# Mixer weights split once and kept in DRAM, and hinted back edges of the block loops

## The chip, the cores and the metric

The kernel runs on one NeuronCore of a Trainium2 chip. The metric is the device time of one execution in microseconds; smaller is better.

## The reference

A hybrid encoder block over 4096 rows of width D = 1024, in fp32. A first layer norm (LN0), then a mixer, a layer norm (LN1), a two-level mixture of experts, and a last layer norm:

```
proj = h @ w_in                       # q 512, k 128, v 128, cb/cc/ch 512 each, gates 2 x 1024
y_attn = window_attention(q, k, v) @ w_attn_out      # chunks of 64, 16 meta tokens, ALiBi, sinks
y_conv = (cb * causal_conv3(cc * ch)) @ w_conv_out
mix = (sigmoid(g_a) * y_attn + sigmoid(g_c) * y_conv) @ w_o
h = LN1(alpha * h + mix)
h = LN2(alpha * h + hier_moe(h))      # router, top 2 of 8 experts in the best of 4 groups
```

Only the mixer is touched by the change.

## The kernel before

`mixer` works through the rows in 8 blocks of 512 (TOK), 4 tiles of 128 each. Each fp32 product is made of three fp32r matmuls: both operands are split into a rounded `hi` part and the rest `lo`, and `hi*hi + hi*lo + lo*hi` is summed in PSUM (`product`, L826 to L828).

The weights of a block are 50 strips of 128 x 1024 floats (0.52 MB): k, v, four q (0 to 5), twelve conv strips cc, ch, cb (6 to 17), then for each of the 8 output columns `ga`, `gc`, `out` (18 to 41), then eight `wo` (42 to 49). A strip is 24 matmuls of 512 columns. Strips 0 to 41 write to the two banks `pj` in turn; an `out` strip writes two products, part 0 to the first bank and part 1 to the second, and the strip behind it writes to the first again. ScalarE takes the products of k, v, q, cc, ga and gc out of the banks, VectorE those of ch, cb and out.

Every engine has its own loop over the blocks and in it the 50 iterations written out in order, so the order of an engine's work is fixed in the program:

- SP (SyncE) loads raw strips into 5 buffers (`load`, L451 to L455). In iteration s it waits for `lo_ready`, that is until the strip four back is split, and loads strip s + 1. In iterations 4 to 7 it then waits for the layer norm LN1 of one row tile and stores that tile to `h1` twice. In iterations 26 to 29 (`X_AT`) it waits for `h_copied` and loads one tile of the next block's `x` (L473).
- ScalarE makes the `hi` part of strip s + 1 in iteration s, once strip s - 1 is done (`strip_done`), after the exponentials of an attention unit where there is one (`split_hi`, L517).
- VectorE makes the `lo` part of strip s + 1 in iteration s, behind the layer norms and attention work of that iteration (`split_lo`, L658), and then takes the strip's products. In iterations 26, 29, 32 and 35 (`LN0_AT`) it begins with a wait for a tile of `x` and measures it for LN0 (L41 to L44); only after that come the split and the products of that strip (for `out`: L767, L769, L771, L774). In iteration 7 of every block an `If` on the block number stands in its program.
- TensorE waits for `lo_ready` before each strip and, for strips that write to `pj`, for the bank to be taken (`pj_taken`).
- GpSimd does the scaling of LN1 and LN0 and the copy of `x` rows into `h`.

`strip_done` counts from 2, so a wait for `b * N + s + 3` holds until strip s of block b is done. The splits use 2 `hi` and 2 `lo` buffers. Before the block loop a first stage normalizes the first block's rows and projects the meta tokens with 5 raw buffers; behind it come the last rows' layer norm, `route` and `experts`.

Of the kernel before, what the change touches and what calls it, by code (L numbers as in the profile page):

```python
# [12 lines left out]
P = 128  # L13
# [40 lines left out]
def mixer(nc, t, x, w_in, w_attn_out, w_conv_out, w_o, h1, logits):  # L54
# [37 lines left out]
    RAW = 5  # L92
    assert N % RAW == 0 and N % 2 == 0
# [35 lines left out]
    with ExitStack() as ctx:  # L129
# [6 lines left out]
        raw = sb("raw", [P, RAW, D])  # L136
        w_hi = sb("w_hi", [P, 2, D], F32R)
        w_lo = sb("w_lo", [P, 2, D], F32R)
# [34 lines left out]
        arena = sb("arena", [P, 2 * KD * TOK])  # L173

        def place(at, name, shape, dt=FP32):
            size = 4 * math.prod(shape[1:])
            assert at[0] + size <= shared + 4 * 2 * KD * TOK
            placed = nc.alloc_sbuf_tensor_at(name, shape, dt, offset=at[0])
            at[0] += size
            return placed  # L180

# [27 lines left out]
        with ExitStack() as c1, nc.Block() as block:  # L209
# [4 lines left out]
            raw_in = [sem1(f"meta_raw_in{i}") for i in range(RAW)]  # L214
# [20 lines left out]
            @block.sync  # L235
            def _(sp):
                def load_strip(n):
                    for dst, src in strip_dmas(*meta_strips[n], raw[:, n % RAW, :]):
                        sp.dma_start(dst, src).then_inc(raw_in[n % RAW], 16)
# [6 lines left out]
                for n in range(1, RAW):  # L246
# [12 lines left out]
                for n in range(RAW, len(meta_strips)):  # L259
                    sp.wait_ge(pj_ready, n - RAW + 1)  # L260
                    load_strip(n)
                sp.wait_ge(consts_in, 16 * (7 + TAPS))
# [104 lines left out]
            @block.tensor  # L367
            def _(pe):
                pe.wait_ge(ident_ready, 1)
                pe.wait_ge(ln_done, 1)  # L370
                for k in range(KD):
                    mm = pe.transpose(tp[0][:, k * META:(k + 1) * META], hm[:, k * P:(k + 1) * P],
                                      ident[0:META, 0:META])
                mm.then_inc(tp_ready, 1)
                uses = [0] * RAW
                for what, n in order:
                    if what == "rows":
                        pe.wait_ge(ln_done, n + 1)
                        for half in range(2):
                            q = 2 * (n - 1) + half  # L380
                            pe.wait_ge(tp_taken_dve, max(1, q))
                            for k in range(4):
                                mm = pe.transpose(tp[q % 2][:, k * P:(k + 1) * P],
                                                  xs[:, n - 1, (4 * half + k) * P:(4 * half + k + 1) * P], ident[:, :])
                            mm.then_inc(tp_ready, 1)
                        continue
                    kind, i = meta_strips[n]
                    uses[n % RAW] += 16 * len(strip_dmas(kind, i, raw[:, 0, :]))
                    pe.wait_ge(raw_in[n % RAW], uses[n % RAW])
                    if n == 0:  # L390
                        pe.wait_ge(tp_taken_dve, 1)
                    if n >= 2:
                        pe.wait_ge(pj_taken, n - 1)
                    for k in range(KD):
                        mm = pe.matmul(pj[n % 2][:, 0:META], raw[:, n % RAW, k * P:(k + 1) * P], hmT[:, k, :],
                                       start=(k == 0), stop=(k == KD - 1))
                    mm.then_inc(pj_ready, 1)
# [4 lines left out]
        h1_out = [sem(f"h1_out{i}") for i in range(TILES)]  # L402
        hi_ready = sem("hi_ready")
# [37 lines left out]
        def raw_uses(s, b):  # L441

            per = lambda ss: 16 * len(strip_dmas(*strips[ss], raw[:, 0, :]))
            slot = s % RAW
            in_block = sum(per(q) for q in range(slot, N, RAW))
            return b * in_block + sum(per(q) for q in range(slot, s + 1, RAW))

        with nc.Block() as block:
            @block.sync
            def _(sp):  # L450
                def load(s, b):  # L451

                    hold(sp, lo_ready, b * N + s + 1)
                    for dst, src in strip_dmas(*strips[s % N], raw[:, s % RAW, :]):
                        sp.dma_start(dst, src).then_inc(raw_in[s % RAW], 16)  # L455

                load(0, 0)
                with sp.Fori(0, BLOCKS) as b:
                    for s in range(N):
                        load(s + 1, b)  # L460
# [7 lines left out]
                        if s in X_AT:  # L468
# [4 lines left out]
                            sp.dma_start(xs[:, i1, :], x[bass.ds(nxt * TOK + i1 * P, P), :]).then_inc(x_in[i1], 16)  # L473
                for i1 in range(TILES):
# [37 lines left out]
            def _(a):  # L512
                def split_hi(b, s):
                    uses = raw_uses(s, b) if s < N else raw_uses(0, b + 1)
                    a.wait_ge(raw_in[s % RAW], uses)
                    a.wait_ge(strip_done, b * N + s + 1)
                    a.activation(w_hi[:, s % 2, :], raw[:, s % RAW, :], ACT.Copy).then_inc(hi_ready, 1)  # L517
# [30 lines left out]
                split_hi(0, 0)  # L548
                with a.Fori(0, BLOCKS) as b:
                    for s, (kind, i) in enumerate(strips):  # L550
# [30 lines left out]
                        split_hi(b, s + 1)  # L581
# [15 lines left out]
                        if s in HX_AT:  # L597
# [4 lines left out]
                             .then_inc(hx_hi, 1)  # L602
                for i in range(TILES):
# [6 lines left out]
            def _(v):  # L610
# [19 lines left out]
                def take_logits(b, block_of):  # L630
# [7 lines left out]
                v.sem_inc(lo_ready, RAW)  # L638
# [5 lines left out]
                v.wait_ge(hi_ready, 1)  # L644
                v.tensor_tensor(w_lo[:, 0, :], raw[:, 0, :], w_hi[:, 0, :].bitcast(FP32), ALU.subtract)\
                 .then_inc(lo_ready, 1)
                with v.Fori(0, BLOCKS) as b:
# [7 lines left out]

                    def split_lo(s):
                        v.wait_ge(hi_ready, b * N + s + 1)
                        v.tensor_tensor(w_lo[:, s % 2, :], raw[:, s % RAW, :], w_hi[:, s % 2, :].bitcast(FP32),  # L658
                                        ALU.subtract).then_inc(lo_ready, 1)
# [18 lines left out]
                    for s, (kind, i) in enumerate(strips):  # L678
# [29 lines left out]
                        if 0 <= n < UNITS:  # L708
# [16 lines left out]
                            if n == 1:  # L725
                                with v.If(b == 0):
                                    v.tensor_copy(bias[0:CHUNK, :, META:PREV], bias_prev[:, :, :])\
                                     .then_inc(prev_set, 1)
# [4 lines left out]
                        split_lo(s + 1)  # L733
# [68 lines left out]
                    assert steps[0] == DVE_STEPS  # L802
                v.wait_ge(wo_taken, BLOCKS * 2 * TILES + 1)
# [19 lines left out]
            def _(pe):  # L823
# [35 lines left out]
                with pe.Fori(0, BLOCKS) as b:  # L859
                    pe.wait_ge(hx_lo, b * 2 * TILES + 1)  # L860
                    for s, (kind, i) in enumerate(strips):
# [27 lines left out]
                        pe.wait_ge(lo_ready, b * N + RAW + s + 1)  # L889
# [3 lines left out]
                        if kind == "wo":  # L893
# [5 lines left out]
                            for tt in range(TILES):  # L899
# [3 lines left out]
                                for k in range(2):  # L903
                                    w = slice(k * TOK, (k + 1) * TOK)
                                    mm = product(quad[tt][:, :], mT_hi[:, 2 * kk + k, toks], mT_lo[:, 2 * kk + k, toks],
                                                 w_hi[:, s % 2, w], w_lo[:, s % 2, w],
# [5 lines left out]
                        else:  # L912
# [4 lines left out]
                            for part, (x_hi, x_lo, k0, ks) in enumerate(parts):  # L917
                                no = out_no[(s, part)]
                                pe.wait_ge(pj_taken[no % 2], b * (NOUT // 2) + no // 2 + 1)
                                for k in range(ks):  # L920
                                    w = slice((k0 + k) * P, (k0 + k + 1) * P)
                                    mm = product(pj[no % 2][:, :], w_hi[:, s % 2, w], w_lo[:, s % 2, w],
# [54 lines left out]
                        if s in HX_AT:  # L977
# [8 lines left out]
                            mm.then_inc(hx_ready, 1)  # L986
                pe.wait_ge(hx_lo, BLOCKS * 2 * TILES + 1)
# [677 lines left out]
```

## Time and profile before

| | us |
|---|---|
| median of 3 runs | 4335.98 (4330.54 to 4336.49) |
| profiled execution, its own time | 4333.28 |
| its span | 4331.5 |
| mean granted TensorE clock | 0.988 |

The page of the profile gives busy time by engine and the costliest groups of instructions. A table by stage gives the same for stretches of the span with the granted clock and the DMA traffic. The timeline lists instructions in order of time, with the idle time before each in brackets and what ended it. "issue" there means that the engine waited for nothing that the profile shows.

### The profile page before, as it was taken

To read this page: it belongs to the slowest core of one execution; us is meant where nothing else is said; L and a number is where in the kernel's file an instruction comes from. 1 tells how busy PE (TensorE), PEld (TensorE's weight loads), DVE (VectorE), ACT (ScalarE), POOL (GpSimd) and SP (SyncE) were. 2 spreads that over 40 slices of the span, in tenths; PEclk is the share of its full clock that TensorE was granted. 3 is DMA by queue.
4 is the path that set the end of the run, shared out by engine and by line. 5 is a ranking of instruction groups with operands and counts; after the bars stand their busy time and mean duration, and the time that the engine had idled before them with its cause. 6 is when DMAs were issued, how large, how long until landed. Compare 5 with 4: busy or idle time off the path is not lost. (4 is left out here: it accounts for less than half of the span.)

```text
span 4331.5 us, 62892 instructions
## 1 busy us (share of the span) xinstructions
PE 4171.0 (96%) x20252; PEld 3428.8 (79%) x20253; DVE 2518.7 (58%) x3263; ACT 1773.0 (41%) x2950; POOL 1094.6 (25%) x1117
## 2 busy tenths in 40 slices
PE   7999999999999999999999999499999999999997
PEld 7887887887887888888888887388788888778886
DVE  5555555555555655645645645777666666765664
ACT  2422422422422422422422422466555555654553
POOL 4022032022022021121121121134333333333333
PEclk9999999999999999999999999799999999999998
DMA  6333333333333333333332332187666666765562
GB/s 171 85 107 103 93 102 98 99 104 97 102 104 89 107 106 85 107 104 89 111 102 80 117 102 78 54 289 248 246 199 198 206 199 234 251 203 198 194 204 90
DMA packets 569472, 601.49 MB, mean 139 GB/s; under 512 B 104080, under 2 KB 426640, under 8 KB 569248
## 3 DMA queue, kind: packets, MB, share of 16 engines
q1 hardware_dynamic: 521152, 476.88, 35.5%
q0 software_dynamic: 48096, 121.71, 8.4%
q8 instruction: 130, 2.13, 0.2%
q14 instruction: 94, 0.77, 0.1%
HBM read 527.15 MB, written 124.78 MB: 151 GB/s over the span
## 5 line engine op out<-in xcount | busy, mean ns | idle before, releaser
L826 PE MATMUL bank<-hT_hi,w_hi 128*128 128x512 f32 x2176 | 864.8, 397 | 30.1 <-DVE w_lo L658 21.3
L658 DVE TENSOR_TENSOR w_lo<-raw,w_hi 128x1024 fp32r<-128x1024 f32 x400 | 597.3, 1493 | 485.5 <-ACT w_hi L517 484.4
L827 PE MATMUL bank<-hT_lo,w_hi 128*128 128x512 f32 x2176 | 850.6, 391 | 2.4 <-issue 2.4
L828 PE MATMUL bank<-hT_hi,w_lo 128*128 128x512 f32 x2176 | 849.2, 390 | 0.0
L1565 PE MATMUL e_bank<-e_w_hi,e_xT_hi 128*128 128x512 f32 x1312 | 521.9, 398 | 14.2 <-DVE e_xT_lo L1488 12.4
L826 PEld LDWEIGHTS bank<-hT_hi,w_hi 128*128 128x128 f32 x2176 | 408.9, 188 | 140.4 <-DVE w_lo L658 32.6
L1567 PE MATMUL e_bank<-e_w_hi,e_xT_lo 128*128 128x512 f32 x1312 | 514.3, 392 | 0.0
L1566 PE MATMUL e_bank<-e_w_lo,e_xT_hi 128*128 128x512 f32 x1312 | 513.4, 391 | 0.0
L1493 DVE TENSOR_TENSOR e_w_lo<-e_raw,e_w_hi 128x1024 fp32r<-128x1024 f32 x384 | 444.4, 1219 | 117.7 <-ACT e_w_hi L1441 110.8
L828 PEld LDWEIGHTS bank<-hT_hi,w_lo 128*128 128x128 f32 x2176 | 408.9, 188 | 87.4
L827 PEld LDWEIGHTS bank<-hT_lo,w_hi 128*128 128x128 f32 x2176 | 409.3, 188 | 86.6 <-issue 5.4
L517 ACT ACTIVATE w_hi<-raw 128x1024 fp32r<-128x1024 f32 x401 | 421.1, 1050 | 12.5 <-PE bank L828 7.9
L1441 ACT ACTIVATE e_w_hi<-e_raw 128x1024 fp32r<-128x1024 f32 x384 | 374.7, 1054 | 18.6 <-DMA e_raw<-in_w_exp_gate_dram 11.1
L1565 PEld LDWEIGHTS e_bank<-e_w_hi,e_xT_hi 128*128 128x128 f32 x1312 | 248.0, 189 | 67.4 <-issue 18.0
L1567 PEld LDWEIGHTS e_bank<-e_w_hi,e_xT_lo 128*128 128x128 f32 x1312 | 247.8, 189 | 53.4
L49 POOL TENSOR_SCALAR rstd<-moments 128x1 f32<-128x1 f32 (+1 forms) x73 | 43.5, 596 | 968.6 <-DVE moments L44 968.6
L1566 PEld LDWEIGHTS e_bank<-e_w_lo,e_xT_hi 128*128 128x128 f32 x1312 | 248.3, 189 | 49.7
L503 POOL COPY h_rows<-x_rows 128x1024 f32<-128x1024 f32 x32 | 33.4, 1044 | 986.7 <-PE bank L838 986.7
L1565 PE MATMUL e_bank<-e_w_hi,e_aT_hi 128*128 128x512 f32 x664 | 266.6, 401 | 2.8 <-DVE e_both L1502 2.7
L1567 PE MATMUL e_bank<-e_w_hi,e_aT_lo 128*128 128x512 f32 x664 | 260.2, 392 | 0.0
L1566 PE MATMUL e_bank<-e_w_lo,e_aT_hi 128*128 128x512 f32 x664 | 259.6, 391 | 0.0
L540 ACT ACTIVATE work<-bank 128x512 f32<-128x512 f32 x128 | 76.6, 599 | 427.6 <-PE bank L828 427.6
(277 smaller groups left out, 7173.3 us busy)
## 6 DMA issues: line engine op xcount, KB each, us to landing
raw<-in_w_in_dram SPq DMA_DIRECT2D x251, 512.0 KB, 3.9
e_raw<-in_w_exp_gate_dram SPq DMA_DIRECT2D x128, 512.0 KB
e_raw<-in_w_exp_up_dram SPq DMA_DIRECT2D x128, 512.0 KB
e_raw<-in_w_exp_down_dram SPq DMA_DIRECT2D x128, 512.0 KB
h_rows<-h_rows SPq DMA_DIRECT2D x72, 512.0 KB, 3.5
raw<-in_w_o_dram SPq DMA_DIRECT2D x64, 512.0 KB, 3.8
raw<-in_w_in_dram SPq DMA_DIRECT2D x64, 256.0 KB, 3.7
raw<-in_w_attn_out_dram SPq DMA_DIRECT2D x64, 256.0 KB, 2.8
```

The source lines that it names most:

```text
L49: po.tensor_scalar(rstd[0:rows, :], moments[0:rows, 1:2], LN_EPS, None, ALU.add).then_inc(ln_rstd, 1)
L517: a.activation(w_hi[:, s % 2, :], raw[:, s % RAW, :], ACT.Copy).then_inc(hi_ready, 1)
L540: a.activation(w[:, 0:TOK], got, ACT.Sigmoid).then_inc(taken_act, 1)
L658: v.tensor_tensor(w_lo[:, s % 2, :], raw[:, s % RAW, :], w_hi[:, s % 2, :].bitcast(FP32), ALU.subtract).then_inc(lo_ready, 1)
L826: pe.matmul(out, hi, x_hi, start=first, stop=False)
L827: pe.matmul(out, hi, x_lo, start=False, stop=False)
L828: return pe.matmul(out, lo, x_hi, start=False, stop=last)
L1441: a.activation(w_hi[:, c, :], raw[:, c, :], ACT.Copy).then_inc(split_count(e, c, True)[0], 1)
L1493: v.tensor_tensor(w_lo[:, c, :], raw[:, c, :], w_hi[:, c, :].bitcast(FP32), ALU.subtract)\
L1565: pe.matmul(out_p, hi, x_hi, start=first, stop=False)
L1566: pe.matmul(out_p, hi, x_lo, start=False, stop=False)
L1567: return pe.matmul(out_p, lo, x_hi, start=False, stop=last)
```

## The change

The hi and lo parts of a strip now stand side by side in a slot (2 x 1024 floats). Block 0 is written out ahead of the loop. In it, raw strips are loaded (3 buffers), split into one of slots 0 to 2 two strips ahead, and each split strip is stored to a DRAM tensor `split_weights` (1.05 MB a strip, 8 KB a partition). Blocks 1 to 7 are a loop without any split: SP loads the split strips from DRAM into 4 slots, three strips ahead of the one that has just been done. The loops of TensorE, ScalarE and VectorE are made with `hint_back_edge=True`; SP's and GpSimd's are as they were. The first stage's raw buffers (`meta_raw`) lie in the same space as the slots.

```diff
+    RAW, META_RAW = 3, 5
+    SLOTS = 4
+    ahead = RAW
+    slot_of = list(range(SLOTS)) * 5 + [0, 1, 2] + list(range(SLOTS)) * 6 + [0, 1, 2]
+    def first_slot(s):
+        return (s + 1) % RAW
...
+        split_d = nc.dram_tensor("split_weights", [N, P, 2 * D], FP32).ap()
...
 # SP
-                def load(s, b):
-                    hold(sp, lo_ready, b * N + s + 1)
-                    for dst, src in strip_dmas(*strips[s % N], raw[:, s % RAW, :]):
+                def load_raw(s):
+                    if s >= RAW:
+                        sp.wait_ge(lo_ready, s - RAW + 1)
+                    for dst, src in strip_dmas(*strips[s], raw[:, s % RAW, :]):
                         sp.dma_start(dst, src).then_inc(raw_in[s % RAW], 16)
+                def store_split(s):
+                    sp.wait_ge(lo_ready, s + 1)
+                    sp.dma_start(split_d[s], slots[first_slot(s)]...).then_inc(w_out[first_slot(s)], 16)
+                def load_split(s, b):
+                    sp.wait_ge(w_out[first_slot(s)], ...)
+                    sp.dma_start(slots[slot_of[s]]..., split_d[s]).then_inc(w_in[slot_of[s]], 16)
-                load(0, 0)
-                with sp.Fori(0, BLOCKS) as b:
+                def block_of_loads(b, first):
                     for s in range(N):
-                        load(s + 1, b)
+                        if first:
+                            store_split(s)
+                        if first and s + ahead < N:
+                            load_raw(s + ahead)
+                        else:
+                            hold(sp, strip_done, b * N + s + 3)
+                            ...
+                            load_split((s + ahead) % N, b + (s + ahead) // N)
                         if s - 3 in LN1_AT:      # stores of h1, as before
                         if s in X_AT:            # load of x, as before
+                for s in range(ahead):
+                    load_raw(s)
+                block_of_loads(0, True)
+                with sp.Fori(1, BLOCKS) as b:
+                    block_of_loads(b, False)
+                for s in range(ahead):
+                    sp.wait_ge(w_in[slot_of[s]], w_uses(s, BLOCKS))
 # ScalarE
-                def split_hi(b, s):
-                    a.wait_ge(strip_done, b * N + s + 1)
+                def split_hi(s):
+                    a.wait_ge(raw_in[s % RAW], raw_uses(s))
+                    if s >= RAW:
+                        a.wait_ge(strip_done, s - RAW + 3)
+                        a.wait_ge(w_out[first_slot(s)], ...)
-                        split_hi(b, s + 1)
+                        if first and s + 2 < N:
+                            split_hi(s + 2)
+                with nc.Fori(1, BLOCKS, engines=bass.OrderedEngineSet([a.engine]), hint_back_edge=True) as b:
+                    block_of_strips(b, False)
 # VectorE
-                            if n == 1:
-                                with v.If(b == 0):
-                                    v.tensor_copy(bias[0:CHUNK, :, META:PREV], bias_prev[:, :, :])\
+                            if n == 1 and first:
+                                v.tensor_copy(bias[0:CHUNK, :, META:PREV], bias_prev[:, :, :]).then_inc(prev_set, 1)
-                        split_lo(s + 1)
+                        if first and s + 2 < N:
+                            split_lo(s + 2)
+                            if i or not first:
+                                v.wait_ge(mlo_ready, b * KD + i)      # in an out strip, before work[2] is written
 # TensorE
-                        pe.wait_ge(lo_ready, b * N + RAW + s + 1)
+                        if first:
+                            pe.wait_ge(lo_ready, s + 1)
+                            w_of = slots[first_slot(s)]
+                        else:
+                            pe.wait_ge(w_in[slot_of[s]], w_uses(s, b))
+                            w_of = slots[slot_of[s]]
...
```

## Rows read from the trace of the kernel before

**Rows 1.** The page's first part: busy us, share of the span, instructions.
```profile
PE 4171.0 (96%) x20252; PEld 3428.8 (79%) x20253; DVE 2518.7 (58%) x3263; ACT 1773.0 (41%) x2950; POOL 1094.6 (25%) x1117
```

**Rows 2.** Table by stage, second block: stretch, length, busy of each engine, clock, DMA.
```profile
391.00:720.00 329.00, 325.05 (x1615) 266.31 (x1613) 179.35 (x241) 107.77 (x198) 61.01 (x36) 1.00 0.35 100
```

**Rows 3.** Waits of TensorE, whole run: total us, times, longest.
```profile
PE bank L826 <- DVE w_lo L658: 21.3, 20, 1.3
```

**Rows 4.** The page's groups of the two splits: busy, mean ns, idle before.
```profile
L658 DVE TENSOR_TENSOR w_lo<-raw,w_hi 128x1024 fp32r<-128x1024 f32 x400 | 597.3, 1493 | 485.5 <-ACT w_hi L517 484.4
...
L517 ACT ACTIVATE w_hi<-raw 128x1024 fp32r<-128x1024 f32 x401 | 421.1, 1050 | 12.5 <-PE bank L828 7.9 <-DMA raw<-in_w_in_dram 4.6
```

**Rows 5.** Timeline of TensorE, second block, sixth and eighth strip: start, length.
```profile
421.52 0.50 PE L826 MATMUL bank<-hT_hi,w_hi 128*128 128x512 f32 x1 [1.12 <-DVE w_lo L658]
421.86 0.39 PE L827 MATMUL bank<-hT_lo,w_hi 128*128 128x512 f32 x1
...
437.78 0.50 PE L826 MATMUL bank<-hT_hi,w_hi 128*128 128x512 f32 x1 [1.26 <-DVE w_lo L658]
```

**Rows 6.** Timeline of TensorE at the back edge into the second block.
```profile
391.19 0.39 PE L828 MATMUL bank<-w_hi,mixT_lo 128*128 128x512 f32 x1
391.65 0.49 PE L826 MATMUL bank<-hT_hi,w_hi 128*128 128x512 f32 x1
...
395.45 0.50 PE L827 MATMUL bank<-hT_lo,w_hi 128*128 128x512 f32 x1 [0.56 <-issue]
...
397.85 0.39 PE L828 MATMUL bank<-hT_hi,w_lo 128*128 128x512 f32 x1
398.33 0.50 PE L826 MATMUL bank<-hT_hi,w_hi 128*128 128x512 f32 x1
```

**Rows 7.** Timeline of VectorE at the same back edge.
```profile
394.66 0.20 DVE L676 COPY kT<-kT 128x64 f32<-128x64 f32 x1 [2.37 <-issue]
```

**Rows 8.** Table by stage: two stores of rows; loads of a strip. Last column GB/s.
```profile
412.00:414.00 2.00, 2.00 (x10) 1.65 (x10) 1.90 (x4) 0.00 (x0) 0.52 (x1) 1.00 1.01 387
563.00:565.00 2.00, 2.00 (x10) 1.41 (x9) 0.00 (x0) 0.00 (x0) 0.00 (x0) 1.00 0.88 235
```

**Rows 9.** Timeline of SP's issues, second block: loads of x and of strips.
```profile
554.40 0.78 SPq L473 DMA_DIRECT2D x_rows<-in_x_dram  x1
561.98 0.37 SPq L455 DMA_DIRECT2D raw<-in_w_in_dram  x1
562.68 0.36 SPq L473 DMA_DIRECT2D x_rows<-in_x_dram  x1
```

**Rows 10.** The tile x_rows, 540 to 600 us, from issue to landing.
```profile
DMA to landing us min/median/max: 4.5/5.1/5.1
```

**Rows 11.** Timeline of VectorE and TensorE around strip 26 of the second block.
```profile
560.67 1.22 DVE L658 TENSOR_TENSOR w_lo<-raw,w_hi 128x1024 fp32r<-128x1024 f32 x1 [0.45 <-ACT w_hi L517]
...
580.87 0.69 DVE L41 BATCH_NORM_STATS2 stats<-x_rows 128x6 f32<-128x512 f32 x1
...
582.26 0.21 DVE L44 BATCH_NORM_AGGREGATE moments<-stats 128x2 f32<-128x12 f32 x1
...
587.08 0.69 DVE L767 TENSOR_TENSOR work<-bank,work 128x512 f32<-128x512 f32 x1
...
589.38 0.40 PE L828 MATMUL bank<-zT_hi,w_lo 128*128 128x512 f32 x1
...
589.81 0.69 DVE L769 TENSOR_TENSOR work<-bank,work 128x512 f32<-128x512 f32 x1 [2.04 <-PE bank L828]
```

**Rows 12.** Behind the last strip: timeline of TensorE; table by stage, clock third from last.
```profile
2696.14 1.94 PE L838 MATMUL bank<-ident,h_rows 128*128 128x128 f32 x8 [5.96 <-DVE h_rows L814]
...
2696.00:2698.00 2.00, 1.86 (x8) 1.57 (x8) 1.86 (x4) 0.60 (x1) 0.41 (x1) 0.50 0.57 229
```

**Rows 13.** Timeline of TensorE at the first block's start: first and tenth matmul.
```profile
62.66 0.79 PE L826 MATMUL bank<-hT_hi,w_hi 128*128 128x512 f32 x1 [7.51 <-DVE w_lo L645]
...
66.66 0.44 PE L826 MATMUL bank<-hT_hi,w_hi 128*128 128x512 f32 x1
```

More of the change, by code:

```diff
@@ L91, in mixer @@
     N = len(strips)
-    RAW = 5
-    assert N % RAW == 0 and N % 2 == 0
+    RAW, META_RAW = 3, 5
+    SLOTS = 4
+    ahead = RAW
+    slot_of = list(range(SLOTS)) * 5 + [0, 1, 2] + list(range(SLOTS)) * 6 + [0, 1, 2]
+    assert N == len(slot_of)
+    def first_slot(s):
+        return (s + 1) % RAW
     CONV0 = 2 + PAIRS
@@ L173, in mixer @@
         arena = sb("arena", [P, 2 * KD * TOK])
+        weights = -(-nc.sbuf_base // 32) * 32
+        weight_space = sb("weight_space", [P, 9 * D])
         def place(at, name, shape, dt=FP32):
             size = 4 * math.prod(shape[1:])
-            assert at[0] + size <= shared + 4 * 2 * KD * TOK
+            assert at[0] + size <= (shared + 4 * 2 * KD * TOK if at[0] < weights else weights + 4 * 9 * D)
             placed = nc.alloc_sbuf_tensor_at(name, shape, dt, offset=at[0])
@@ L180, in place @@
             return placed
+        at = [weights]
+        slots = [place(at, f"w_slot{i}", [P, 2, D], F32R) for i in range(SLOTS)]
+        raw = place([weights + 4 * 6 * D], "raw", [P, RAW, D])
+        meta_raw = place([weights + 4 * 4 * D], "meta_raw", [P, META_RAW, D])
         at = [shared]
@@ L213, in mixer @@
             gains_in = sem1("gains_in")
-            raw_in = [sem1(f"meta_raw_in{i}") for i in range(RAW)]
+            raw_in = [sem1(f"meta_raw_in{i}") for i in range(META_RAW)]
             ln_step, ln_moments, ln_rstd, ln_gained, ln_done = (
@@ L237, in load_strip @@
                 def load_strip(n):
-                    for dst, src in strip_dmas(*meta_strips[n], raw[:, n % RAW, :]):
-                        sp.dma_start(dst, src).then_inc(raw_in[n % RAW], 16)
+                    for dst, src in strip_dmas(*meta_strips[n], meta_raw[:, n % META_RAW, :]):
+                        sp.dma_start(dst, src).then_inc(raw_in[n % META_RAW], 16)
                 sp.dma_start(hm, t["meta"]).then_inc(meta_in, 16)
@@ L245, in _ @@
                 sp.dma_start(xs[:, :, :], x[0:TOK, :].rearrange("(t p) d -> p t d", p=P)).then_inc(x_in, 16)
-                for n in range(1, RAW):
+                for n in range(1, META_RAW):
                     load_strip(n)
@@ L258, in _ @@
                     sp.dma_start(dst, row.unsqueeze(0).to_broadcast([P, row.shape[0]])).then_inc(consts_in, 16)
-                for n in range(RAW, len(meta_strips)):
-                    sp.wait_ge(pj_ready, n - RAW + 1)
+                for n in range(META_RAW, len(meta_strips)):
+                    sp.wait_ge(pj_ready, n - META_RAW + 1)
                     load_strip(n)
@@ L374, in _ @@
                 mm.then_inc(tp_ready, 1)
-                uses = [0] * RAW
+                uses = [0] * META_RAW
                 for what, n in order:
@@ L394, in _ @@
                     for k in range(KD):
-                        mm = pe.matmul(pj[n % 2][:, 0:META], raw[:, n % RAW, k * P:(k + 1) * P], hmT[:, k, :],
+                        mm = pe.matmul(pj[n % 2][:, 0:META], meta_raw[:, n % META_RAW, k * P:(k + 1) * P], hmT[:, k, :],
                                        start=(k == 0), stop=(k == KD - 1))
@@ L402, in mixer @@
         h1_out = [sem(f"h1_out{i}") for i in range(TILES)]
+        w_in = [sem(f"w_in{i}") for i in range(SLOTS)]
+        w_out = [sem(f"w_out{i}") for i in range(RAW)]
         hi_ready = sem("hi_ready")
@@ L439, in mixer, with raw_uses, w_uses @@
         LNS = 2 * TILES
[L441 to L446, printed above, removed]
+        def raw_uses(s):
+            return sum(16 * len(strip_dmas(*strips[q], raw[:, 0, :])) for q in range(s % RAW, s + 1, RAW))
+        def w_uses(s, b):
+            slot = slot_of[s]
+            return 16 * ((b - 1) * slot_of.count(slot) + slot_of[0:s + 1].count(slot))
         with nc.Block() as block:
@@ L450, in _ @@
             def _(sp):
-                def load(s, b):
-                    hold(sp, lo_ready, b * N + s + 1)
-                    for dst, src in strip_dmas(*strips[s % N], raw[:, s % RAW, :]):
+                def load_raw(s):
+                    if s >= RAW:
+                        sp.wait_ge(lo_ready, s - RAW + 1)
+                    for dst, src in strip_dmas(*strips[s], raw[:, s % RAW, :]):
                         sp.dma_start(dst, src).then_inc(raw_in[s % RAW], 16)
-                load(0, 0)
-                with sp.Fori(0, BLOCKS) as b:
-                    for s in range(N):
-                        load(s + 1, b)
+                def store_split(s):
+                    sp.wait_ge(lo_ready, s + 1)
+                    sp.dma_start(split_d[s], slots[first_slot(s)][:, :, :].rearrange("p h d -> p (h d)").bitcast(FP32))\
+                      .then_inc(w_out[first_slot(s)], 16)
+                def load_split(s, b):
+                    sp.wait_ge(w_out[first_slot(s)], 16 * (sum(first_slot(q) == first_slot(s) for q in range(s + 1))))
+                    sp.dma_start(slots[slot_of[s]][:, :, :].rearrange("p h d -> p (h d)").bitcast(FP32), split_d[s])\
+                      .then_inc(w_in[slot_of[s]], 16)
+                def block_of_loads(b, first):
+                    for s in range(N):
+                        if first:
[5 more added lines that the diff above has]
+                            if first:
+                                sp.wait_ge(w_out[first_slot(s)],
+                                           16 * (sum(first_slot(q) == first_slot(s) for q in range(s + 1))))
+                            load_split((s + ahead) % N, b + (s + ahead) // N)
                         if s - 3 in LN1_AT:
@@ L512, in _ @@
             def _(a):
-                def split_hi(b, s):
-                    uses = raw_uses(s, b) if s < N else raw_uses(0, b + 1)
-                    a.wait_ge(raw_in[s % RAW], uses)
-                    a.wait_ge(strip_done, b * N + s + 1)
-                    a.activation(w_hi[:, s % 2, :], raw[:, s % RAW, :], ACT.Copy).then_inc(hi_ready, 1)
+                def split_hi(s):
+                    a.wait_ge(raw_in[s % RAW], raw_uses(s))
+                    if s >= RAW:
+                        a.wait_ge(strip_done, s - RAW + 3)
+                        a.wait_ge(w_out[first_slot(s)], 16 * (sum(first_slot(q) == first_slot(s) for q in range(s))))
+                    a.activation(slots[first_slot(s)][:, 0, :], raw[:, s % RAW, :], ACT.Copy).then_inc(hi_ready, 1)
                 def take(b, s):
@@ L546, in take_rows, with block_of_strips @@
                      .then_inc(rt_act, 1)
-                split_hi(0, 0)
-                with a.Fori(0, BLOCKS) as b:
+                def block_of_strips(b, first):
                     for s, (kind, i) in enumerate(strips):
@@ L602, in _ @@
                              .then_inc(hx_hi, 1)
+                for s in range(2):
+                    split_hi(s)
+                block_of_strips(0, True)
+                with nc.Fori(1, BLOCKS, engines=bass.OrderedEngineSet([a.engine]), hint_back_edge=True) as b:
+                    block_of_strips(b, False)
                 for i in range(TILES):
@@ L643, in _, with split_lo, block_of_strips @@
                 v.sem_inc(hx_lo, 1)
[L644 to L647, printed above, removed]
+                def split_lo(s):
+                    slot = slots[first_slot(s)]
+                    v.wait_ge(hi_ready, s + 1)
+                    v.tensor_tensor(slot[:, 1, :], raw[:, s % RAW, :], slot[:, 0, :].bitcast(FP32),
+                                    ALU.subtract).then_inc(lo_ready, 1)
+                def block_of_strips(b, first):
                     steps = [0]
@@ L654, in link @@
                         v.wait_ge(dve_step, b * DVE_STEPS + steps[0])
[L656 to L659, printed above, removed]
                     def output(s, part=0):
@@ L802, in _ @@
                     assert steps[0] == DVE_STEPS
+                for s in range(2):
+                    split_lo(s)
+                block_of_strips(0, True)
+                with nc.Fori(1, BLOCKS, engines=bass.OrderedEngineSet([v.engine]), hint_back_edge=True) as b:
+                    block_of_strips(b, False)
                 v.wait_ge(wo_taken, BLOCKS * 2 * TILES + 1)
@@ L857, in router_logits, with block_of_strips @@
                     mm.then_inc(lg_ready, 1)
-                with pe.Fori(0, BLOCKS) as b:
+                def block_of_strips(b, first):
                     pe.wait_ge(hx_lo, b * 2 * TILES + 1)
@@ L887, in _ @@
                             mm.then_inc(s_ready, 1)
-                        pe.wait_ge(lo_ready, b * N + RAW + s + 1)
+                        if first:
+                            pe.wait_ge(lo_ready, s + 1)
[3 more added lines that the diff above has]
+                            w_of = slots[slot_of[s]]
                         if kind == "out" and i == 0:
@@ L905, in _ @@
                                     mm = product(quad[tt][:, :], mT_hi[:, 2 * kk + k, toks], mT_lo[:, 2 * kk + k, toks],
-                                                 w_hi[:, s % 2, w], w_lo[:, s % 2, w],
+                                                 w_of[:, 0, w], w_of[:, 1, w],
                                                  kk == 0 and k == 0, kk == 3 and k == 1)
@@ L921, in _ @@
                                     w = slice((k0 + k) * P, (k0 + k + 1) * P)
-                                    mm = product(pj[no % 2][:, :], w_hi[:, s % 2, w], w_lo[:, s % 2, w],
+                                    mm = product(pj[no % 2][:, :], w_of[:, 0, w], w_of[:, 1, w],
                                                  x_hi[:, k, :], x_lo[:, k, :], k == 0, k == ks - 1)
@@ L986, in _ @@
                             mm.then_inc(hx_ready, 1)
+                block_of_strips(0, True)
+                with nc.Fori(1, BLOCKS, engines=bass.OrderedEngineSet([pe.engine]), hint_back_edge=True) as b:
+                    block_of_strips(b, False)
                 pe.wait_ge(hx_lo, BLOCKS * 2 * TILES + 1)
```

9 lines of the change are left out of this document (2 added, 7 removed).

## The prediction

> **What bounds the kernel now.** I read the page's head first, then a table by stage, then who waits for whom, and last the order of time at the places that the change touches. TensorE is busy for 4171 of 4331.5 us [rows 1], and the table by stage shows the mixer's block loop as eight nearly equal stretches of 328 us in which TensorE is busy for 324, VectorE for 179 and ScalarE for 108 [rows 2]. So the mixer is bound by TensorE's own stream. Within a strip its matmuls start 0.227 us apart, whatever the others do; 24 of them make a strip of 5.45 us. Work that leaves VectorE or ScalarE is worth only the places where TensorE stands still for them. The list of waits names them: 21.3 us in 20 waits for `w_lo` (L658) over the whole run [rows 3]. A modelled matmul lasts 0.39 us and the next starts after 0.227, so a stall is longer than its idle time by 0.16; I measure from start to start.
>
> **What the change removes.** In blocks 1 to 7 both splits go: 1.05 us on ScalarE and about 1.5 us on VectorE for each of 350 strips [rows 4], some 370 and 520 us of engine time, priced at nothing in itself, because TensorE covers it. What TensorE gets back, per block:
> - Sixth strip. 1.12 us idle for `w_lo`, 1.28 from start to start beyond 0.227, and 0.11 more because the second matmul follows after 0.34 [rows 5]: 1.4 us.
> - Eighth strip. 1.26 us behind the first attention unit, which ScalarE's exponentials and then both splits hold up; the usual start would be 0.07 earlier than the modelled end: 1.3 us [rows 5].
> - Block start. 391.19 to 391.65, 394.50 to 395.45 (released by "issue", so the sequencer had no instruction) and 397.85 to 398.33, each with the slow second matmul: 0.33 + 0.82 + 0.35 = 1.5 us [rows 6]. The last of them is VectorE, which itself lost 2.37 us to "issue" at its back edge before it came to split [rows 7]; that one goes for certain. The other two go only as far as the hint brings the loop's first instructions in time. No row shows a hinted edge; the bounds are 0.35 and 1.5 us, and I take 1.0.
>
> That is 3.7 us times 7 = 26 us. Block 0 still splits, but two strips ahead instead of one, which covers the first two places there too: 2.7 us. Sum 28.5 us, with bounds 22 and 38 (the upper one adds the 0.85 us before the V transposes, which wait for the copy of the last q on ScalarE).
>
> The Trainium skill ("Runtime: NRT & Kernel Launch", section Instruction fetch mechanics) says that a taken branch whose target is out of the fetched window stalls until a DMA has brought it, and knows no hint. If that held for a hinted branch too, block starts would give 0.35 us each, and the time would be, as an estimate, 5 us above my sum. The 0.95 us step on TensorE agrees that something is fetched there; no run here shows a hinted branch.
>
> **What the change adds: transfers.** A strip becomes one load of 1.05 MB instead of 0.52. The nearest stretch with long packets, two stores of tile rows (1.05 MB), moves 387 GB/s, and a stretch of strip loads in 512-byte packets 235 [rows 8]. At 387 the load takes 2.7 us, at 235 4.5, both under the strip's 5.45, and it is asked for two strips ahead. I price it at nothing; the cover is gone if transfers fall under 192 GB/s (1.05 MB in 5.45 us). Block 0 moves 1.57 MB per strip (read plus store), 4.1 us at 387: hidden, bounds 0 and 20 us for that block. `h1` stores: in the new order SP comes to iterations 4 to 7 only when those strips are done, later than the layer norm of the tile it waits for, so that wait no longer holds loads. The extra `mlo_ready` wait on VectorE names an instruction three strips old: nothing. The three loads beyond the last block land while VectorE normalizes the last rows: nothing, at most 1 us. Removing the `If` frees VectorE, not TensorE.
>
> **What the change moves: SP's whole queue.** This decides the sign. Before, SP waited for `lo_ready` four strips back, so it ran about four strips ahead, and everything else in its program ran ahead with it. Now SP's iteration s first holds for `strip_done` of strip s itself. The loads were re-aimed (s + 3), but the load of `x` stands where it stood, in iterations 26 to 29, and VectorE asks for tile 0 at the start of its iteration 26, before it takes strip 26's products out of the two `pj` banks. Strip 27 needs the bank of strip 26's first part. The circle is: strip 26 done, SP loads strip 29, SP loads `x`, `x` lands, VectorE measures, VectorE multiplies, TensorE may begin strip 27. Before, `x` was asked for at 554.40 and measured at 580.87, 26 us apart, before strip 26 had begun [rows 9, 11]. Behind the waiting VectorE stand both products of strip 26, and behind those ScalarE's `mixT_hi` and TensorE.
>
> The price from rows, counted from the start of strip 26's last matmul (589.38):
> - to strip_done and VectorE's reaction 0.43 (L769 at 589.81) [rows 11]; SP's reaction 0.1 more (L658 ends at 561.89, SP issues at 561.98) [rows 9, 11];
> - from the first issue to the landing of `x`: 0.70 between the two issues, then 4.5 to 5.1 to landing, 5.1 the median [rows 9, 10]. There 0.52 MB in 512-byte packets stand ahead of it, some 2 us; now 1.05 MB in long ones, 2.7: 6.4 us, bounds 5.2 and 8.0;
> - L41, L42 and L44: 580.87 to 582.47, 1.60 us; the first product L767 0.69; three hand-overs of about 0.1 [rows 11].
>
> 0.53 + 6.4 + 1.6 + 0.7 + 0.25 = 9.5 us; less the 0.227 due anyway, plus 0.11 for the slow second matmul: 9.4 us. Seven blocks: 66 us (bounds 55 and 80). Tile 1 costs nothing: it is asked for when strip 27 is done, lands about 6.5 us later and has to be measured by the middle of strip 29. Block 0 pays nothing either: there SP still follows `lo_ready`, two strips ahead.
>
> The Trainium skill ("DMA: Bandwidth & Descriptors", section Bandwidth) has 6.15 us for a transfer of 1 MB. By it, as an estimate, `x` would land 3.5 us later, and the time would be 24 us above my sum. The trace speaks against it: two 0.52 MB stores at 387 GB/s.
>
> Then the clock. A stop of 5.96 us after the last strip ends with TensorE at a granted 0.50, which is 1.2 GHz, though it had run without a pause before [rows 12]. At the start of the loop, after 7.51 us of idling, nine steps from matmul to matmul take 4.00 us, 0.44 each, before the 0.227 of 2.4 GHz sets in [rows 13]; nine at 0.227 would take 2.0 us, so 2.0 us are lost. A stop of 9.4 us is longer than both, so I add 2.0 us per block, 14 us, bounds 0 and 24.
>
> **Sum.** +66 + 14 - 28.5 = +51 us on the profiled execution's 4333.28 us (span 4331.5 plus 1.8 around it): 4385 us. The profiled execution lies 2.7 us under the median of the runs and inside their spread.
>
> **Rivals.**
> - A. `x` isn't exposed, the change is faster: 4333 - 28.5 = 4305 us. It decides if `x` is there before strip 27's turn, so if VectorE gets past its iteration 26 without the tile. For it: 26 us of lead before. Against it: the lead came from SP running ahead, and the order of the program closes the circle. A chance of 0.07.
> - B. The stop is there, the clock holds 2.4 GHz: 4371 us. For it: the drop is granted by a rule that I see only from outside; against: both longest stops of this engine beside the loop ended at 1.2 GHz. 0.13.
> - C. Transfers bind as well: if the 1.05 MB loads share their time with the `x` rows and SP's issue so that strip loads miss two or three strips in a block by 2 us each, 4385 + 35 = 4420 us. For it: twice the bytes; against: 387 GB/s. 0.08.
> - D. The gain is larger and the stop shorter (38 and 7 x 7): 4333 + 49 - 38 = 4344 us, 8 us from the median of the runs and so just no change. 0.03.
>
> The forecast has 0.69.
>
> **How the numbers follow.** No change is within 0.2%, about 9 us. The forecast, B and C are slower, 0.90; D is taken as the same, 0.03; A is faster, 0.07. The bounds of the terms give 4333 + 55 + 0 - 38 = 4350 and 4333 + 80 + 24 - 22 = 4415. All at one end together is unlikely, and C reaches to 4420, so the range is 4352 to 4416.
>
> **What would show it.** In blocks 1 to 7 TensorE should stand still once per block for some 9 us ahead of the strip after the third `out` strip, released by VectorE's product of that strip (L767's successor), behind a VectorE wait for the DMA of `x_rows`; SP's issue of `x` should come about 1 us after strip 26's last matmul; the granted clock should read 0.5 just behind. The waits for `w_lo` should be gone, block 0 without a stop. If the stop is missing, the sign is wrong; if waits for the slot loads appear, C; if matmuls keep 0.227 behind the stop, B.

## The result, and the profile after

The changed kernel takes 4381.09 us (median of 4 runs, 4378.87 to 4385.46) against 4333.26 us: a ratio of 1.0111, 95% interval 1.0094 to 1.0129. It is slower by 48 us. The forecast was 4385 us, 51 us above the profiled execution of the kernel before. The profiled execution took 4378.95 us, its span is 4376.3.

The head of the page and a table by stage (blocks 0, 1 and 2; busy time of TensorE, its weight loads, VectorE, ScalarE, GpSimd; clock, DMA share, GB/s), after:

```profile
PE 4174.4 (95%) x20252; PEld 3444.1 (79%) x20253; DVE 1989.7 (45%) x2912; ACT 1440.0 (33%) x2598; POOL 1020.1 (23%) x1117
```
```profile
64.00:389.00 325.00, 323.57 (x1608) 266.86 (x1607) 177.01 (x239) 103.88 (x194) 59.76 (x36) 1.00 0.80 256
389.00:725.00 336.00, 324.97 (x1613) 267.72 (x1613) 103.84 (x190) 60.45 (x147) 49.44 (x36) 0.99 0.51 181
725.00:1059.00 334.00, 324.79 (x1613) 267.97 (x1612) 103.87 (x190) 60.45 (x147) 49.47 (x36) 0.98 0.50 177
```

VectorE has lost 529 us of work against [rows 1], and in a block 75 of its 179 us [rows 2]; TensorE is as busy as before, and the block is 6 us longer. The clock column is the first hint: 0.98 where [rows 2] has 1.00.

The waits of TensorE, and one of VectorE, after (total us, times, longest):

```profile
PE bank L884 <- DVE work L819: 60.5, 8, 8.6
PE bank L884 <- DMA w_slot<-split_weights: 1.8, 1, 1.8
```
```profile
DVE stats L41 <- DMA x_rows<-in_x_dram: 198.5, 16, 17.0
```

The `w_lo` wait of [rows 3] is gone. In its place stands one of 8.6 us for L819, the first product of an `out` strip (L767 before), and behind that VectorE's wait for `x`, 0.2 us in the whole run before. The timeline around strip 26 of block 2, first TensorE and VectorE, then SP's issues, then the tile's time to landing:

```profile
918.49 0.40 PE L886 MATMUL bank<-zT_hi,w_slot 128*128 128x512 f32 x1
927.41 0.80 PE L884 MATMUL bank<-hT_hi,w_slot 128*128 128x512 f32 x1 [8.52 <-DVE work L819]
```
```profile
925.07 0.69 DVE L41 BATCH_NORM_STATS2 stats<-x_rows 128x6 f32<-128x512 f32 x1 [16.93 <-DMA x_rows<-in_x_dram]
...
926.46 0.21 DVE L44 BATCH_NORM_AGGREGATE moments<-stats 128x2 f32<-128x12 f32 x1
926.66 0.69 DVE L819 TENSOR_TENSOR work<-bank,work 128x512 f32<-128x512 f32 x1
```
```profile
918.97 0.32 SPq L485 DMA_DIRECT2D w_slot<-split_weights  x1
919.71 0.34 SPq L512 DMA_DIRECT2D x_rows<-in_x_dram  x1
```
```profile
DMA to landing us min/median/max: 5.3/5.4/5.5
```

Read it as a circle. The last matmul of strip 26 starts at 918.49. SP issues the strip load 0.48 us later and `x` 0.74 us after that. `x` lands 5.4 us later and VectorE measures it at 925.07, where before it had measured it 26 us after the issue [rows 9, 11]. Then come 1.6 us of measuring and 0.7 for the product, and strip 27 starts at 927.41, 8.92 us after its predecessor's last matmul instead of 0.227. Behind it the clock:

```profile
927.50:931.00 3.50, 3.50 (x9) 2.73 (x10) 2.56 (x4) 0.63 (x1) 0.33 (x2) 0.50 0.00 0
```

A granted 0.50 is 1.2 GHz; the steps from matmul to matmul there are 0.427 us, about the 0.44 of [rows 13].

**Where the 44.8 us of span went.** From the timelines I take the block loop as the time from the first strip's first matmul to the last strip's last one: 62.66 to 2689.80 before, 61.96 to 2731.27 after, so 2627.1 and 2669.3 us. Ahead of it 0.7 us are gained, behind it 3.3 lost (1641.7 and 1645.0 us). A block from start to start took 328.4 us before and 334.35 after (blocks 2 to 6).

### The profile page after: what moved, and what is told of

The parts are those of the page before. It is cut to its first block and busy times, and to the rows that moved or that the text cites. A ratio compares the mean times of both kernels' runs of the same rounds, so it can differ in the third digit from the quotient of the medians.

```text
span 4376.3 us, 60798 instructions
## 1 busy us (share of the span) xinstructions
PE 4174.4 (95%) x20252; PEld 3444.1 (79%) x20253; DVE 1989.7 (45%) x2912; ACT 1440.0 (33%) x2598; POOL 1020.1 (23%) x1117
## 5 line engine op out<-in xcount | busy, mean ns | idle before, releaser
L884 PE MATMUL bank<-hT_hi,w_slot 128*128 128x512 f32 x2176 | 869.9, 400 | 69.5 <-DVE work L819 60.5
L885 PE MATMUL bank<-hT_lo,w_slot 128*128 128x512 f32 x2176 | 854.8, 393 | 0.0
L886 PE MATMUL bank<-hT_hi,w_slot 128*128 128x512 f32 x2176 | 853.5, 392 | 0.0
L884 PEld LDWEIGHTS bank<-hT_hi,w_slot 128*128 128x128 f32 x2176 | 412.6, 190 | 173.3 <-DVE work L819 62.9
L886 PEld LDWEIGHTS bank<-hT_hi,w_slot 128*128 128x128 f32 x2176 | 412.2, 189 | 88.9
L885 PEld LDWEIGHTS bank<-hT_lo,w_slot 128*128 128x128 f32 x2176 | 413.2, 190 | 82.6
L49 POOL TENSOR_SCALAR rstd<-moments 128x1 f32<-128x1 f32 (+1 forms) x73 | 28.2, 386 | 1045.3 <-DVE moments L44 1045.3
L819 DVE TENSOR_TENSOR work<-bank,work 128x512 f32<-128x512 f32 x64 | 44.3, 692 | 361.7 <-PE bank L886 361.4
L884 PE MATMUL bank<-w_slot,mixT_hi 128*128 128x512 f32 x512 | 205.6, 402 | 0.0
```

What stands on the lines that cost most here:

```text
L884: pe.matmul(out, hi, x_hi, start=first, stop=False)
L885: pe.matmul(out, hi, x_lo, start=False, stop=False)
L886: return pe.matmul(out, lo, x_hi, start=False, stop=last)
```

## The experiments

The time of one execution scatters by up to 0.3% around the median on the chips of these runs. What lies behind the loop took between 1640.7 and 1652.0 us in the eleven profiles. So for each kernel the loop's length from its profile stands beside the ratio to the kernel before (2627.1 us).

| kernel | median us | ratio, 95% interval | loop, us |
|---|---|---|---|
| changed | 4381.09 | 1.0111, 1.0094 to 1.0129 | 2669.3 |
| x_early | 4303.38 | 0.9937, 0.9919 to 0.9954 | 2591.8 |
| x_first | 4365.37 | 1.0084, 1.0068 to 1.0101 | 2647.7 |
| before_x_late | 4410.84 | 1.0173, 1.0155 to 1.0191 | 2704.2 |
| fill | 4360.79 | 1.0057, 1.0038 to 1.0075 | 2655.3 |
| ln0_late | 4305.41 | 0.9932, 0.9911 to 0.9953 | 2594.8 |
| before_hint | 4316.00 | 0.9966, 0.9954 to 0.9977 | 2614.6 |
| x_early_nohint | 4307.25 | 0.9941, 0.9922 to 0.9960 | 2603.3 |
| x_early_pehint | 4304.53 | 0.9933, 0.9917 to 0.9950 | 2591.7 |
| early_stores | 4298.60 | 0.9925, 0.9910 to 0.9940 | 2589.9 |

### x_early: is the load of x the whole loss?

```diff
-        X_AT = {MIX0 + 8 + i: i for i in range(TILES)}
+        X_AT = {MIX0 + 4 + i: i for i in range(TILES)}
```

> The changed kernel with SP's loads of x moved from iterations 26 to 29 to iterations 22 to 25; nothing else. My theory (the whole loss is the circle through the x load, with the slow clock behind it): the stop of 8.9 us before strip 27 and its nine slow matmuls go in blocks 1 to 7, 7 x 10.8 = 75 us, and the 0.9 us in block 0: 4381 - 76 = 4305 us, faster than the kernel before by 28 us. Rival (the doubled bytes or the longer instruction stream cost something by themselves): the stop goes, but the time stays above 4330 us. Rival (VectorE is late at strip 26 for another reason, x only the last of its waits): a stop remains there under another name, 4350 us or more.

The time fell to 4303.38 us. The wait for L819 is gone, the loop is 77.5 us shorter, and a block takes 323.54 us, the same to 0.01 us in five blocks. The table by stage for block 3 and VectorE's timeline, x_early:

```profile
1036.00:1359.50 323.50, 322.81 (x1613) 266.76 (x1612) 103.75 (x190) 60.45 (x147) 49.47 (x36) 1.00 0.52 182
```
```profile
1218.58 0.31 DVE L686 TENSOR_TENSOR logits<-bank,router_bias 128x144 f32 x1 [2.64 <-PE bank L913]
1218.81 0.68 DVE L41 BATCH_NORM_STATS2 stats<-x_rows 128x6 f32<-128x512 f32 x1
```

VectorE goes from the router's logits to the tile without waiting. The transfers are the same bytes (182 GB/s) and cost nothing in the steady blocks, so both rivals fall.

### ln0_late: the circle cut at its other side

```diff
-        LN0_AT = {MIX0 + 8 + 3 * i: i for i in range(TILES)}
+        LN0_AT = {MIX0 + 11 + 3 * i: i for i in range(TILES)}
```

> The changed kernel with the load of x left where it is (iterations 26 to 29) and VectorE's measuring of the x tiles moved from iterations 26, 29, 32, 35 to 29, 32, 35, 38: the same circle broken at its other side. My theory: x is asked for when strip 26 is done and lands 6 us later, half way through strip 28 at the latest, VectorE asks for it at strip 29: no stop, block loop within 3 us of the one with x loaded early (2592 us), 4381 - 77 = 4304 us. Rival (the load of x behind strip 26 hurts in itself, by its traffic or by holding SP's queue): 10 us or more above that.

4305.41 us, and blocks 2 to 6 take 323.54 us again. The loop is 3.0 us longer than x_early's, in blocks 0 and 1 alone. Block 0 begins with eleven steps of 0.427 us instead of five. In block 1 the wait for a slot load lasts 2.56 us from start to start, against 2.43 in x_early, and here eight steps of 0.427 us follow, there none. Neither lies at the load of `x`. SP's load of `x` may stay where the change left it; what counts is the distance between the strip whose end SP holds for and the iteration in which VectorE needs the tile.

### before_x_late: the stop without any split weights

```diff
                             i1 = X_AT[s]
+                            if i1 == 0:
+                                hold(sp, strip_done, b * N + s + 3)
                             hold(sp, h_copied, b * TILES + i1 + 1)
```

> The kernel before, with one wait more: SP holds for strip_done of strip 26 ahead of the load of tile 0 of x, as the changed kernel does in effect; splits and bytes as before. My theory: the stop appears in all eight blocks without any part of the split weights: 0.53 + landing 4.2 + 1.6 measuring + 1.2 for the split of strip 27, which stands behind the measuring, + hand-overs = 7.5 to 8.5 us, and 2.0 us of slow clock: 8 x 10 = +80 us, 4413 us (4400 to 4425). Rival (the stop needs the new transfers or the slots): under 4350 us.

One wait on SP in the kernel before costs 77.1 us in the loop. The waits of TensorE, before_x_late:

```profile
PE bank L828 <- DVE work L769: 57.6, 8, 7.3
PE bank L828 <- DVE w_lo L660: 22.2, 22, 1.3
```

Eight stops of 7.5 to 7.7 us from start to start, with the `w_lo` waits of [rows 3] left in place. The stop needs neither the slots nor the new transfers.

### x_first: the length of the stop

```diff
+                    def load_x(s):                 # the wait for h_copied and the load, as before
...
+                            if s in X_AT and not first:
+                                load_x(s)
                             load_split((s + ahead) % N, b + (s + ahead) // N)
...
-                        if s in X_AT:
...
+                        if s in X_AT and first:
+                            load_x(s)
```

> The changed kernel with the load of x issued ahead of the strip load in the same iteration (blocks 1 to 7), both still behind strip 26. My theory of the stop's length (issue, landing behind 1.05 MB, measure, product): x is issued 0.65 us earlier and has no 1.05 MB ahead of it, 2.6 us at 400 GB/s, so the stop falls from 8.9 to about 5.8 us; the clock still falls in a stop of that length: 4381 - 7 x 3.2 = 4359 us. If the packets of both loads share the engines instead of queueing in order, x lands only 0.7 to 1.5 us earlier: 4371 to 4376 us. If the clock does not fall in 5.8 us, 4346 us.

The loop is 21.6 us shorter, 22 expected; the time, 4365.37 us, lies between the 4359 expected and the 4371 of the rival in which both loads share the engines. SP and VectorE in block 3, x_first, and the tile's time to landing:

```profile
1248.11 0.34 SPq L493 DMA_DIRECT2D x_rows<-in_x_dram  x1
1248.50 0.42 SPq L485 DMA_DIRECT2D w_slot<-split_weights  x1
1251.21 0.69 DVE L41 BATCH_NORM_STATS2 stats<-x_rows 128x6 f32<-128x512 f32 x1 [14.30 <-DMA x_rows<-in_x_dram]
```
```profile
DMA to landing us min/median/max: 3.1/3.3/3.6
```

With nothing ahead of it, `x` lands in 3.3 us instead of 5.4, though 1.05 MB follow 0.39 us behind: the 1.05 MB ahead had cost 2.1 us. The loop decides against loads that share the engines, which would have gained 0.7 to 1.5 us a block; 3.1 came. The stop is 6.3 to 6.5 us, longer than the 5.8 expected, because SP issues `x` 0.84 us behind strip 26's last matmul (1247.27), only 0.4 us earlier than in the changed kernel. The clock still falls, for fewer steps: 5 or 6 of 0.427 us in blocks 3 to 7, against 8 or 9 in the changed kernel.

### fill: the clock

```diff
+                                if not first and s == MIX0 + 9:
+                                    for _ in range(38):
+                                        pe.matmul(quad[3][:, :], w_of[:, 0, 0:P], hT_hi[:, 0, :],
+                                                  start=True, stop=True)
                                 pe.wait_ge(pj_taken[no % 2], b * (NOUT // 2) + no // 2 + 1)
```

> The changed kernel with 38 matmuls of 512 columns into an unused PSUM bank, put ahead of the wait for the bank of strip 27 in blocks 1 to 7 (8.6 us at 0.227 us each); their result is not used. My theory (the granted clock falls because TensorE stands still): the clock stays at 2.4 GHz, the nine slow matmuls go, 7 x 1.9 = 13 us: 4368 us. Rival (the slow matmuls have another cause, such as the transfers landing at that moment): 4381 us or a little more.

The filled stretch of block 3, fill (columns as above), and what follows it:

```profile
1250.00:1256.00 6.00, 6.00 (x28) 4.98 (x27) 1.07 (x2) 0.00 (x0) 0.00 (x0) 1.00 0.61 246
1256.00:1262.00 6.00, 5.84 (x26) 4.49 (x26) 3.83 (x7) 0.63 (x1) 2.04 (x3) 1.00 0.00 0
```
```profile
1257.28 0.50 PE L884 MATMUL bank<-hT_hi,w_slot 128*128 128x512 f32 x1 [0.16 <-DVE work L819]
```

The clock stays at 1.00, which is 2.4 GHz, no step behind the stretch takes 0.427 us, and the loop is 14.0 us shorter. Of these 13.4 lie in blocks 1 to 7, 1.9 us a block: the price of the clock that falls when TensorE stands still. The transfers are the same, so the rival falls. The time fell by 20 us at the median, but the profiled execution by 8; the loop is the sure part.

### The hints: before_hint, x_early_nohint, x_early_pehint

before_hint is the kernel before with

```diff
-                with pe.Fori(0, BLOCKS) as b:
+                with nc.Fori(0, BLOCKS, engines=bass.OrderedEngineSet([pe.engine]), hint_back_edge=True) as b:
```

on TensorE, and the same on ScalarE and VectorE. The other two take hints out of x_early again, on all three engines or on all but TensorE.

> The kernel before with hinted back edges on TensorE, ScalarE and VectorE and nothing else. Theory: the block starts lose what the hint can give (1.5 to 1.7 us in 7 block changes), the w_lo waits at the sixth and eighth strip stay; at the exit of the loop the hinted engines stand still for instructions, 2 us on VectorE and 2 to 4 on TensorE, as the changed kernel shows: the block loop is 11 us shorter, what follows 3 us longer, 4331 - 8 = 4323 us. Rival (a hint changes nothing, the block starts were gained by taking the splits out of VectorE's way): only the gaps released by w_lo change, none of the issue gaps, 4331 us.

> The changed kernel with x loaded in iterations 22 to 25 and with plain back edges on all engines. Theory: TensorE stands still at each of 6 back edges (blocks 1 to 7) for the 0.3 and 0.8 us of the kernel before, 6 x 1.2 = 7 us more in the loop than with hints; behind the loop the 3 to 5 us of the exit come back: 4303 + 7 - 4 = 4306 us. Rival (hints do nothing, or their exit costs nothing): loop and tail each as with hints.

> The changed kernel with x loaded in iterations 22 to 25 and with a hinted back edge on TensorE alone. Theory: VectorE no longer feeds weights in the loop, so its back edge is hidden and its hint only costs 1.8 us at the exit: block loop as with three hints, 2592 us, the first row tile of the last layer norm 1.8 us earlier: 4301 us. Rival (VectorE's back edge still holds TensorE): the loop is 6 x 0.4 us or more longer.

Hints alone make the kernel before faster, 0.9966, and its loop 12.5 us shorter. The back edge into block 2, TensorE and VectorE, before_hint:

```profile
717.79 0.39 PE L828 MATMUL bank<-w_hi,mixT_lo 128*128 128x512 f32 x1
718.01 0.39 PE L826 MATMUL bank<-hT_hi,w_hi 128*128 128x512 f32 x1
718.24 0.39 PE L827 MATMUL bank<-hT_lo,w_hi 128*128 128x512 f32 x1
```
```profile
718.82 0.19 DVE L676 COPY kT<-kT 128x64 f32<-128x64 f32 x1
```

The matmuls go through the edge at 0.227 us where [rows 6] have 0.46, 0.95 and 0.48, and VectorE's 2.37 us for "issue" [rows 7] are gone; the `w_lo` waits of the sixth and eighth strip stay (18.2 us in 16 waits). So the rival falls. Without hints the edge in the new loop costs again (x_early_nohint, block 3):

```profile
1039.49 0.49 PE L884 MATMUL bank<-hT_hi,w_slot 128*128 128x512 f32 x1 [1.16 <-issue]
```

and the loop is 11.5 us longer, where 7 were expected: a plain edge costs 1.9 us here, not 1.2. Without hints the new loop is still 23.8 us shorter than the one before: that much the splits' going is worth by itself. x_early_pehint has x_early's loop to 0.1 us: VectorE's and ScalarE's hints gain nothing once they feed no weights.

The exits came out partly otherwise; of the 3 us expected behind the loop in before_hint 1.1 came. Behind the loop the changed kernel stands still for instructions, first VectorE, then TensorE:

```profile
2737.98 1.28 DVE L872 SCALAR_TENSOR_TENSOR h_rows<-h_rows,rstd,ln_bias 128x1024 f32<-128x1024 f32 x1 [2.64 <-issue]
```
```profile
2750.00 2.56 PE L904 MATMUL bank<-router_rowsT,router_weights 128*36 128x128 f32 x11 [3.79 <-issue]
```

From the last matmul of the loop to the router's last transposes it takes 37.7 us, before 30.9; 37.3 in x_early, 34.5 and 36.0 in the two runs with TensorE's hint alone (x_early_pehint, early_stores), 31.4 without hints. But before_hint, hinted on all three, takes 32.0 and shows neither stall. So the hint costs something at the exit of this program and not of that one. Where in the instruction stream an exit has to lie for that, no run tells; it stays open.

### early_stores: the one late slot

Besides x_early_pehint's edits:

```diff
-                        if first:
-                            store_split(s)
+                        if first and s <= N - ahead:
+                            for q in (range(s, N) if s == N - ahead else (s,)):
+                                store_split(q)
```

> x loaded in iterations 22 to 25, a hint on TensorE alone, and the stores of split strips 47 to 49 in block 0 issued together ahead of the first wait for strip_done. Theory of the one wait for a slot load in block 1 (2.1 us before the third strip): the stores of strips 48 and 49 stood behind SP's holds, so the slots came free late and with them the loads; now the wait goes, block loop 2590 us instead of 2592, about 4301 us. Rival (block 0's traffic is the limit there): the wait stays.

The wait for `w_slot<-split_weights` is gone with the same bytes moved, so the rival falls. In x_early SP had issued the store of strip 49 at 384.53 and the next slot load, which waits for that store to land, only at 394.64. Block 1 now takes 323.54 us as the others, and the loop is the shortest of all, 2589.9 us. With 4298.60 us at a ratio of 0.9925 it is the fastest version run, and faster than both kernels; against x_early and x_early_pehint its interval overlaps, so that order rests on the loop alone.

## Why the prediction was right

- **The stop (66 us, 9.4 a block).** Right in place, order and releasers. Measured 8.92 us from start to start, 8.7 more than due, so 61 us. The landing was 0.3 us too long (0.74 + 5.4 = 6.1 us instead of 6.4; the 1.05 MB ahead of `x` cost 2.1 us, 2.7 had been taken), the reactions and hand-overs 0.3, and the 0.11 for a slow second matmul is already in the slow clock.
- **The clock (14 us).** Right: x_early shortens a block by 10.8 us, 8.7 is the stop, 2.1 is left; fill gives 1.9 a block by itself. Rival B falls.
- **What TensorE gets back (28.5 us).** Too small. A block of x_early is 4.8 us shorter than one before, 3.7 were taken. Matmul by matmul over one block, the lead grows by 1.7 us at the block start, 1.4 at the sixth strip, 1.4 at the eighth, and 0.3 at a place that I had not seen. The step that was mis-sized is the block start: the hint gives all of it, 1.7 us, where the upper bound was 1.5 and 1.0 was taken. Over seven blocks 33.8 us, with block 0's 2.6 in the changed kernel 36.
- **Block 0 pays nothing.** Wrong by 0.9 us: `x`, behind a store and a load there, was late there too; that is the eighth wait for L819, and it went with x_early.
- **Transfers at nothing.** Right in the steady blocks, at 0.5 of the DMA engines. Block 1 had one wait of 2.0 us for a slot, which was not priced; early_stores puts it down to the order of SP's stores and not to the bytes. Rival C falls otherwise.
- **Loop exits.** Not in the sum. Up to the router's last transposes 6.8 us were lost, behind the loop as a whole 3.3; what lies there varies by more than that from profile to profile.

The loop's change adds up: 7 x 10.8 + 0.9 + 2.0 - 33.8 - 2.6 = +42.1 us; measured are 2669.3 - 2627.1 = 42.2. The mechanism was right. That the total came within 4 us of the median, and 6 us of the profiled execution, is in part luck: a stop 5 us too long and a gain 8 us too small, both in the direction of too slow, were half made up for by the exit, the slot and block 0, which were not in the sum. Rival A was the right description of x_early: 4305 us, measured 4303.

## What to carry to other kernels

When a queue's trigger is moved, list every DMA and wait in that engine's program, not only the transfer it was moved for: here three strips of lead were kept for the weights and lost for `x`, and one line that moved `x` by four iterations turned 1.1% slower into 0.6% faster. Taking 529 us of work off VectorE was worth only what TensorE waited for it, some 3 us a block. A stop is to be priced with the slow clock behind it, here a quarter more.

## What the runs showed of the hardware

- A hinted back edge cost TensorE nothing that its 0.227 us step shows (before_hint); a plain one cost 1.8 us in the kernel before (12.5 us in 7 edges) and 1.9 in x_early_nohint (11.5 in 6).
- With hints, leaving the loop cost VectorE 2.64 and TensorE 3.79 us of "issue" in the changed kernel and nothing in before_hint.
- In block 0 a store of 1.05 MB took 4.5 to 10.1 us to land while strip loads ran beside it, at 256 GB/s and 0.80 of the DMA engines. TensorE lost 0.9 us there to a late `x`, and none with the same bytes and `x` asked for four iterations earlier (x_early). It lost 2.0 us at the first slots of block 1, and none with the same bytes and the last three stores ahead of the first hold (early_stores).
- Stops of 8.9 us (changed kernel), 7.6 (before_x_late) and 6.4 (x_first) all ended at 1.2 GHz, followed by 5 to 12 steps of 0.427 us. Of the single waits in block 1, the one of 2.56 us in ln0_late was followed by a granted 0.52 and eight such steps, the one of 2.43 in x_early by 1.00 and none.
